# Second attention: each head's query and key halves stacked in 128 rows, one product pair and one wait per head

## The chip, the cores and the metric

One NeuronCore of a Trainium2 chip runs the whole program. The metric is the device time in microseconds (us) of one execution; lower is better. TensorE is written PE (PEld for its weight loads), VectorE DVE, ScalarE ACT, GpSimd POOL, and SP is the engine that issues most transfers.

## What is computed

The reference is two transformer blocks on 512 tokens of width 1024. The change lies in the attention of the second block (`fox_attention`), with 16 heads of size 64:

```python
def fox_attention(h, w_in, b_f, w_out):
    proj = h @ w_in
    q, k, v = ...                       # 16 heads of 64, from proj
    q = q * jnp.asarray(HEAD_DIM_2 ** -0.5, q.dtype)
    f_logit = (proj[..., 3 * D:] + b_f).astype(jnp.float32)
    log_f = jax.nn.log_sigmoid(f_logit)
    c = lax.cumsum(log_f, axis=1).transpose(0, 2, 1)
    ...
        s = jnp.einsum('bhqd,bhkd->bhqk', qb, k, preferred_element_type=jnp.float32)
        s = s + cb[..., :, None] - c[..., None, :]
        s = jnp.where(k_pos[None, :] <= q_pos[:, None], s, NEG_INF)
        pr = jax.nn.softmax(s, axis=-1)
    ...
    return o @ w_out
```

The term `cb` is the same for all keys of a query, so softmax drops it. The kernel adds only the sums of the gate that belong to the keys (`c`).

## The kernel before

Every matrix product is made of three products of rounded parts: a value is split into a "hi" part (fp32r) and a "lo" rest, and hi*hi + hi*lo + lo*hi are added in PSUM. Weights come in 352 transfers of 512 KB, one for each unit of 128 x 1024: SP loads it into `w_raw`, ACT rounds it into `w_hi` (function `highs`), POOL subtracts to get `w_lo`, and PE multiplies (lines 519 to 521, helper `three`). A unit fills one PSUM bank. All engines run hand-written instruction lists that wait on counting semaphores, so the order in the code is the order on each engine.

The second attention works on 8 pairs of heads, `fox_pair(p)`, one for each 128 output columns. Units `fox + 3p`, `+1`, `+2` make q, k and v of pair p. They are made ahead, in the gaps of earlier pairs: `more(i)` (or `fill`) puts the table `FOX_FILL[p][i]` pieces of 3 products of 128x512 between the steps of the attention. When a unit is complete, ACT and DVE evict it at the same index i, in `fox_evict(p, i)`: DVE multiplies by the inverse norm (`fox_scaled`), ACT writes the hi part (`fox_high`, after one weight rounding by `highs`), and DVE writes the lo part at its next `evict` (`fox_low`). By the table q of a later pair is evicted in pairs 0 (i = 3), 1 (3), 2 (5), 3 (7), 4 (10) and 6 (0), k in pairs 0 (7), 1 (9), 3 (0), 4 (1), 5 (2) and 6 (4), and v of the last pair at the very end of pair 6 (i = 11). Units 3 to 5 are complete before pair 0 starts.

In a pair, the scores of query block qi (0 to 3) against (qi + 1) x 128 keys go to PSUM bank 2 for head 0 and bank 3 for head 1 (`scores(qi)`). The two heads lie in rows 0 to 63 and 64 to 127 of the same tiles. There are four products with 64 rows for each head: q_hi k_hi, q_hi k_lo, q_lo k_hi, and ones with `c_head`, which holds the gate's sums of the pair in one row of each half. Then a causal mask is added by a product with the identity (line 984). DVE takes the row maxima (`peak`, line 1320), ACT the exponentials with their sums (`exps`, line 1991), DVE divides (`normalise`). PE turns the probabilities (line 1000), ACT and DVE split them (`fpt_hi`, `fpt_lo`), and PE multiplies them by v (`pv`, lines 1007 to 1009). `head_rows(p)` on DVE writes `c_head` of the next pair after the last `normalise`. `CREDIT` is a start value of 2 on some semaphores. Pair 7 has no units to make; it fills with pieces of the output product (`fill_out`).

Ahead of pair 0, ACT and DVE work out the gate: the absolute value, exponential and logarithm on ACT, the running sum `c_rows` on DVE, mixed with the first q, k and v.

## Time and profile before

| what | value |
|---|---|
| three runs | 2181.66 us median, 2180.15 to 2186.51 |
| the profiled execution | 2185.68 us, span 2183.9 us |
| PE busy | 2146.1 us, 98% of the span |
| DVE, ACT, POOL busy | 1013.6, 869.6, 933.8 us |
| mean granted TensorE clock | 0.994 |
| weight transfers | 352 of 512 KB, 3.5 us each to landing |

PE is busy nearly all the time, so the program's length is PE's instruction list plus the holes in it. The second attention lies between about 885 and 1115 us of the span. The first score product of the eight pairs starts at 900.86, 928.87, 955.92, 982.08, 1008.58, 1034.51, 1061.87 and 1088.33 us.

### The profile page before, as it was taken

The page shows a single profiled execution, that of the slowest core. Times are in us where ns is not written, and L with a number is a line of the kernel's source. Part 1 is how long each engine was busy: PE and PEld are TensorE (multiplying, and loading weights), DVE is VectorE, ACT ScalarE, POOL GpSimd, SP SyncE. Part 2 cuts the span into 40 slices and gives each one's busy share as a digit, 9 for nine tenths or more (in the row PEclk, how much of TensorE's full clock was granted, in tenths as well). Part 3 has the DMA queues.
Part 4 walks back from the last instruction along what each step waited for, and adds up shares of the span by engine and source line. Part 5 has one row for each costly group of instructions (what it writes and reads, how often), then busy time and mean ns, then how long its engine had stood idle before and what let it go on. Part 6 is the DMA issues. An engine that isn't in the chain of part 4 may idle for free.

```text
span 2183.9 us, 25305 instructions
## 1 busy us (share of the span) xinstructions
PE 2146.1 (98%) x10192; PEld 1758.8 (81%) x10192; DVE 1013.6 (46%) x1637; ACT 869.6 (40%) x1358; POOL 933.8 (43%) x424
## 2 busy tenths in 40 slices
PE   9999999999999999999999999999999999999998
PEld 7877778888888887777778888888888888888886
DVE  5877775445524235666634422313653345122134
ACT  5434346444424254444434422324532244233234
POOL 5722124434444455322225444444554454444446
PEclk9999999999999999999999999999999999999999
DMA  4421112233233332211122333322223323332222
GB/s 159 148 75 41 47 49 80 94 97 106 97 97 97 97 115 78 70 57 49 49 67 88 97 97 97 97 97 87 97 87 97 97 85 99 97 97 96 97 80 85
DMA packets 53829, 193.27 MB, mean 88 GB/s; under 512 B 6096, under 2 KB 6224, under 8 KB 53712
## 3 DMA queue, kind: packets, MB, share of 16 engines
q1 hardware_dynamic: 52992, 189.81, 27.0%
q10 hardware_dynamic: 720, 1.84, 0.3%
q8 instruction: 81, 1.33, 0.2%
q14 instruction: 36, 0.29, 0.0%
HBM read 189.53 MB, written 2.10 MB: 88 GB/s over the span
## 4 chain that ended last, share of the span: by engine, by line
PE 89%; DVE 6%; ACT 3%; issue 1%; DMA 0%; POOL 0%; DVEq 0%; ACTq 0%; POOLq 0%
PE ps L519 27%; PE ps L521 27%; PE ps L520 27%; PE ps L733 1%; DVE ps L1209 1%; PE ps L982 1%; PE ps L713 1%; PE ps L1000 1%; PE ps L725 1%; ACT w_hi L1855 1%; PE ps L615 1%; DVE xg_lo L1169 1%; PE ps L1007 0%; DVE ps L1730 0%; PE ps L715 0%
## 5 line engine op out<-in xcount | busy, mean ns | idle before, releaser
L472 POOL TENSOR_TENSOR w_lo<-w_raw,w_hi 128x1024 fp32r<-128x1024 f32 x352 | 852.6, 2424 | 1211.4 <-ACT w_hi L1855 1211.3
L519 PE MATMUL ps<-xg_hi,w_hi 128*128 128x512 f32 x1688 | 674.1, 399 | 5.4 <-POOL w_lo L486 2.8
L521 PE MATMUL ps<-xg_hi,w_lo 128*128 128x512 f32 x1688 | 661.2, 392 | 0.0
L520 PE MATMUL ps<-xg_lo,w_hi 128*128 128x512 f32 x1688 | 660.7, 391 | 0.0
L1855 ACT ACTIVATE w_hi<-w_raw 128x1024 fp32r<-128x1024 f32 x352 | 372.3, 1058 | 626.5 <-PE ps L521 623.8
L519 PEld LDWEIGHTS ps<-xg_hi,w_hi 128*128 128x128 f32 x1688 | 318.8, 189 | 69.3 <-issue 3.0
L521 PEld LDWEIGHTS ps<-xg_hi,w_lo 128*128 128x128 f32 x1688 | 318.5, 189 | 67.9
L520 PEld LDWEIGHTS ps<-xg_lo,w_hi 128*128 128x128 f32 x1688 | 319.2, 189 | 59.4
L521 PE MATMUL ps<-h_hi,w_lo 128*128 128x512 f32 x688 | 267.8, 389 | 0.0
L519 PE MATMUL ps<-h_hi,w_hi 128*128 128x512 f32 x688 | 267.8, 389 | 0.0
L520 PE MATMUL ps<-h_lo,w_hi 128*128 128x512 f32 x688 | 267.8, 389 | 0.0
L1143 DVE TENSOR_TENSOR ps<-ps,inv_rms 128x512 f32<-128x512 f32 x164 | 113.6, 696 | 194.2 <-PE ps L521 181.1
L521 PEld LDWEIGHTS ps<-h_hi,w_lo 128*128 128x128 f32 x688 | 129.2, 188 | 26.9
L520 PEld LDWEIGHTS ps<-h_lo,w_hi 128*128 128x128 f32 x688 | 129.2, 188 | 26.7
L519 PEld LDWEIGHTS ps<-h_hi,w_hi 128*128 128x128 f32 x688 | 129.2, 188 | 26.6
L1499 DVE TENSOR_TENSOR mixed<-mixed,ps 128x512 f32<-128x512 f32 x48 | 33.0, 688 | 199.9 <-PE ps L521 199.9
L1169 DVE SCALAR_TENSOR_TENSOR xg_lo<-resid,vec,xg_hi 128x512 fp32r<-128x512 f32 x72 | 85.5, 1191 | 12.7 <-ACT xg_hi L1881 12.5
L1209 DVE SCALAR_TENSOR_TENSOR ps<-glu,vec,ps 128x512 f32<-128x512 f32 x116 | 87.1, 751 | 1.9
L1844 ACT ACTIVATE h_hi<-ps 128x512 fp32r<-128x512 f32 x86 | 51.5, 598 | 90.1 <-DVE ps L1761 48.8
L1881 ACT ACTIVATE xg_hi<-resid,vec 128x512 fp32r<-128x512 f32 x72 | 51.7, 717 | 62.7 <-DVE resid L1499 40.2
L481 POOL TENSOR_TENSOR sq_sum<-sq_sum,sq 128x512 f32<-128x512 f32 x42 | 66.2, 1577 | 23.7 <-ACT sq L1878 21.4
L1761 DVE TENSOR_TENSOR ps<-tile_b,ps 128x512 f32<-128x512 f32 x64 | 44.6, 696 | 57.7 <-ACT tile_b L2296 57.7
(342 smaller groups left out, 2462.7 us busy)
## 6 DMA issues: line engine op xcount, KB each, us to landing
w_raw<-in_weights SPq DMA_DIRECT2D x352, 512.0 KB, 3.5
out_x<-mixed SPq DMA_DIRECT2D x8, 256.0 KB, 2.1
resid<-in_x SPq DMA_DIRECT2D x3, 512.0 KB, 7.4
p_raw<-in_p ACTq DMA_DIRECT2D x3, 512.0 KB, 3.6
resid<-in_x SPq DMA_DIRECT2D x2, 256.0 KB, 4.0
last_gain<-in_last_gain SPq DMA_DIRECT2D x1, 512.0 KB, 4.6
w_raw<-in_weights SPq DMA_DIRECT2D x1, 256.0 KB, 4.0
w_raw<-in_weights ACTq DMA_DIRECT2D x1, 256.0 KB, 4.4
```

The costliest lines, as they stand in the source:

```text
L472: pool.tensor_tensor(w_lo[:, slot, :], w_raw[:, u % RAW, :], w_hi[:, slot, :].bitcast(F32), ALU.subtract).then_inc(w_ready, 1)
L481: pool.tensor_tensor(sq_sum[:], sq_sum[:], sq[:, m % 2:m % 2 + 1, :], ALU.add).then_inc(summed, 1)
L519: pe.matmul(o, w, x, start=start, stop=False)
L520: pe.matmul(o, w, xl, start=False, stop=False)
L521: return pe.matmul(o, wl, x, start=False, stop=stop)
L1143: dve.tensor_tensor(out, ps[:, BANK[u]:BANK[u] + 1, :], R[:], ALU.mult).then_inc(done, 1)
L1169: dve.scalar_tensor_tensor(xg_lo[:, m:m + 1, :], X[:, m:m + 1, :], g, xg_hi[:, m:m + 1, :].bitcast(F32), ALU.mult, ALU.subtract).then_inc( ...
L1209: ins = dve.scalar_tensor_tensor(acc if k < CONV_TAPS - 1 else conv_acc[:, ct, :], src, w, acc, ALU.mult, ALU.add)
L1761: dve.tensor_tensor(t, T2[:, m % 2:m % 2 + 1, :], t, ALU.mult).then_inc(s_mlp["s"], 1)
L1844: act.activation(out, x, ACT.Copy, scale=scale).then_inc(done, 1)
L1855: act.activation(w_hi[:, u % RING, :], w_raw[:, u % RAW, :], ACT.Copy).then_inc(w_hi_ready, 1)
L1881: act.activation(xg_hi[:, m:m + 1, :], X[:, m:m + 1, :], ACT.Copy, scale=g).then_inc(prep_hi, 1)
```

## The change

For each head there is a stack of 128 rows. In `fq[.., hd, t]` the head's own 64 rows hold q_hi for both t = 0 and t = 1; the other 64 rows hold ones for t = 0 and q_lo for t = 1. In `fk[.., hd, t]` the own rows hold k_hi (t = 0) and k_lo (t = 1); the other rows hold the gate's sums (t = 0) and a copy of k_hi (t = 1). Product t = 0 is q_hi k_hi plus ones times sums, product t = 1 is q_hi k_lo plus q_lo k_hi. So a head has two products with 128 rows instead of four with 64. Each head's products and mask now stand together and wait for the exponentials of that head alone.

To fill the stacks, ACT writes q_hi as two instructions of 64x1024 and k_hi as two of 64x512, and issues two transfers that copy k_hi to the other half (128 KB each, two for each pair, at the place of the v unit). DVE writes q_lo, k_lo and the gate's sums as two instructions of 64 rows each. The ones are written once by four ACT instructions ahead of the gate. There is no `c_head`; its content lies in the double-buffered `fk`.

```diff
-            for n, (first, base) in enumerate(((0, 0), (32, 0), (64, -1), (96, -1))):
+            for n, (first, base) in enumerate(((0, -1), (32, -1), (64, 0), (96, 0))):
...
                 def scores(qi):
                     e, n = 8 * p + 2 * qi, (qi + 1) * P
-                    pe.wait_ge(A2["exps"], e + 2)
                     qs = slice(qi * P, n)
-                    for t, (a, b) in enumerate(((q[0][:, qs], k[0]), (q[0][:, qs], k[1]), (q[1][:, qs], k[0]), (ones_r, c_head))):
-                        for hd in range(2):
-                            rows = slice(hd * HD, (hd + 1) * HD)
-                            pe.matmul(ps[:, 2 + hd, 0:n], a[rows, :], b[rows, 0:n], start=t == 0, stop=False)
                     for hd in range(2):
+                        pe.wait_ge(A2["exps"], e + hd + 1)
+                        for t in range(2):
+                            pe.matmul(ps[:, 2 + hd, 0:n], fq[:, par, hd, t, qs], fk[:, par, hd, t, 0:n], start=t == 0, stop=False)
                         pe.matmul(ps[:, 2 + hd, qs], ident_r[:], causal_r[:], start=False, stop=True).then_inc(A2["scores"], 1)
...
-                pe.wait_ge(A2["crow"], p + 1)
+                pe.wait_ge(A2["qklo"], 2 * p + 2)
+                pe.wait_ge(A2["crow"], 2 * p + 2)
+                pe.wait_ge(A2[f"kdup{par}"], 32 * (p // 2 + 1))
+                if p == 0:
+                    pe.wait_ge(A2["ones"], 4)
                 scores(0); more(0)
...
             def fox_low(n):
                 if which == 0:
-                    dve.wait_ge(A2["qkhi"], 2 * p + 1)
-                    dve.scalar_tensor_tensor(fq_lo[:, par:par + 1, :], bank(u0 + n), HD ** -0.5, fq_hi[:, par:par + 1, :].bitcast(F32),
-                                             ALU.mult, ALU.subtract).then_inc(bank_free, 1)
+                    dve.wait_ge(A2["qkhi"], 4 * p + 2)
+                    for hd, done in ((0, A2["qklo"]), (1, bank_free)):
+                        rows, other = (slice(h * HD, (h + 1) * HD) for h in (hd, 1 - hd))
+                        dve.scalar_tensor_tensor(fq[other, par, hd, 1, :], ps[rows, BANK[u0 + n], :], HD ** -0.5,
+                                                 fq[rows, par, hd, 1, :].bitcast(F32), ALU.mult, ALU.subtract).then_inc(done, 1)
...
             def head_rows(p):
-                dve.tensor_scalar(c_head[:], c_rows[:], head_sel[:, p:p + 1], None, ALU.mult).then_inc(A2["crow"], 1)
+                for hd in range(2):
+                    other = slice((1 - hd) * HD, (2 - hd) * HD)
+                    dve.tensor_scalar(fk[other, p % 2, hd, 0, :], c_rows[other, :], head_sel[other, p:p + 1], None,
+                                      ALU.mult).then_inc(A2["crow"], 1)
...
             def fox_high(n):
                 highs(u0 + n + 1 + RING)
                 if which < 2:
                     act.wait_ge(A2["qk"], 2 * p + which + 1)
-                    copy_hi((fq_hi, fk_hi)[which][:, par:par + 1, :], bank(u0 + n), A2["qkhi"], (HD ** -0.5, 1.0)[which])
+                for hd in range(2):
+                    rows, other = (slice(h * HD, (h + 1) * HD) for h in (hd, 1 - hd))
+                    if which == 0:
+                        copy_hi(fq[rows, par, hd, :, :], ps[rows, BANK[u0 + n], :].unsqueeze(1).to_broadcast([HD, 2, S]), A2["qkhi"], HD ** -0.5)
+                    elif which == 1:
+                        copy_hi(fk[rows, par, hd, 0, :], ps[rows, BANK[u0 + n], :], A2["qkhi"])
+                    else:
+                        if hd == 0:
+                            act.wait_ge(A2["qkhi"], 4 * p + 4)
+                        act.dma_start(fk[other, par, hd, 1, :].bitcast(F32), fk[rows, par, hd, 0, :].bitcast(F32)).then_inc(A2[f"kdup{par}"], 16)
+            for par in range(2):
+                for hd in range(2):
+                    other = slice((1 - hd) * HD, (2 - hd) * HD)
+                    copy_hi(fq[other, par, hd, 0, :].rearrange("p (a b) -> p a b", b=P), ones[other, :].unsqueeze(1).to_broadcast([HD, QB, P]),
+                            A2["ones"])
             taken(U["forget"])
```

On PE, before, `scores(3)` of pair 0 stands like this, behind the pieces of `more(2)` (a row's number is its place on the engine; the shapes printed are those of the output):

```order
3947 L521 MATMUL ps<-xg_hi,w_lo 128x512
3948 L982 MATMUL ps<-fk_hi,fq_hi 128x512 [waits fox_exps]
3949 L982 MATMUL ps<-fk_hi,fq_hi 128x512
3950 L982 MATMUL ps<-fk_lo,fq_hi 128x512 x2
3951 L982 MATMUL ps<-fk_hi,fq_lo 128x512 x2
3952 L982 MATMUL ps<-c_head,ones_r 128x512 x2
3953 L984 MATMUL ps<-causal_r,ident_r 128x128 x2
3954 L519 MATMUL ps<-xg_hi,w_hi 128x512
```

The same place of the changed kernel:

```order
3947 L518 MATMUL ps<-xg_hi,w_lo 128x512
3948 L977 MATMUL ps<-fk,fq 128x512 [waits fox_exps]
3949 L977 MATMUL ps<-fk,fq 128x512
3950 L978 MATMUL ps<-causal_r,ident_r 128x128
3951 L977 MATMUL ps<-fk,fq 128x512 [waits fox_exps]
3952 L977 MATMUL ps<-fk,fq 128x512
3953 L978 MATMUL ps<-causal_r,ident_r 128x128
3954 L516 MATMUL ps<-xg_hi,w_hi 128x512
```

Eight products of half height for both heads have become four of full height, and head 0's mask stands ahead of head 1's products.

On ACT, before, from the end of the norm that precedes the stage up to the first exponentials of pair 0 (`inv_rms` is the norm, `logf` the gate, `fprob` the probabilities):

```order
508 L1889 ACTIVATE inv_rms<-ps 128x512 [waits norm_broadcast]
509 L2217 ACTIVATE logf<-logf,vec 128x512 [waits bank_free]
510 L2219 ACT_TABLE_LOAD
511 L2219 ACTIVATE logf<-logf 128x512 [waits forget_act]
512 L1844 ACTIVATE fq_hi<-ps 128x512 [waits fox_qk]
513 L1844 ACTIVATE fk_hi<-ps 128x512 [waits fox_qk]
514 L2223 ACT_TABLE_LOAD
515 L2223 ACTIVATE logf<-logf,ones 128x512 [waits forget_act]
516 L2226 ACTIVATE c_hi<-c_rows 128x512 [waits forget_dve]
518 L1844 ACTIVATE fq_hi<-ps 128x512 [waits fox_qk]
520 L1844 ACTIVATE fk_hi<-ps 128x512 [waits fox_qk]
523 L1991 ACTIVATE fprob,fstat<-ps,fstat 128x128 [waits fox_peak] x2
```

And of the changed kernel, up to the gate's logarithm and the first two transfers:

```order
508 L1894 ACTIVATE inv_rms<-ps 128x512 [waits norm_broadcast]
509 L1849 ACTIVATE fq<-ones 64x512 x4
510 L2236 ACTIVATE logf<-logf,vec 128x512 [waits bank_free]
511 L2238 ACT_TABLE_LOAD
512 L2238 ACTIVATE logf<-logf 128x512 [waits forget_act]
513 L1849 ACTIVATE fq<-ps 64x1024 [waits fox_qk]
514 L1849 ACTIVATE fq<-ps 64x1024
515 L1849 ACTIVATE fk<-ps 64x512 [waits fox_qk]
516 L1849 ACTIVATE fk<-ps 64x512
518 L2242 ACTIVATE logf<-logf,ones 128x512 [waits forget_act]
519 L2227 DMA fk<-fk 64x512 [waits fox_qkhi]
520 L2227 DMA fk<-fk 64x512
```

Four instructions for the ones stand ahead of the gate's first step, and the first q and k, ahead of its last step, have become four longer or equal ones.

On ACT at the border of pairs 6 and 7, in the changed kernel (before, the same rows stood there without the two transfers):

```order
687 L1849 ACTIVATE fo_hi<-ps 64x512 [waits fox_pv]
688 L1860 ACTIVATE w_hi<-w_raw 128x1024 [waits w_loaded2,unit_done]
689 L2227 DMA fk<-fk 64x512 [waits fox_qkhi]
690 L2227 DMA fk<-fk 64x512
691 L1996 ACTIVATE fprob,fstat<-ps,fstat 128x128 [waits fox_peak] x2
```

The transfers for pair 7 stand behind a weight rounding that waits for the last unit PE makes in pair 6.

## Rows read from the trace of the kernel before

**Rows 1.** The page's chain that ended last, by engine.

```profile
PE 89%; DVE 6%; ACT 3%; issue 1%; DMA 0%; POOL 0%; DVEq 0%; ACTq 0%; POOLq 0%
```

**Rows 2.** Windows: busy us and instructions by engine, clock, pair 2.

```profile
955.80:982.00 26.20, 26.20 (x152) 20.71 (x151) 16.20 (x40) 12.07 (x31) 6.45 (x3) 1.00 0.20 61
```

**Rows 3.** Timeline of PE, pair 2, `scores(3)`: start, duration, engine, line.

```profile
964.26 0.39 PE L521 MATMUL ps<-xg_hi,w_lo 128*128 128x512 f32 x1
964.58 0.50 PE L982 MATMUL ps<-fk_hi,fq_hi 64*128 64x512 f32 x2
964.91 0.39 PE L982 MATMUL ps<-fk_lo,fq_hi 64*128 64x512 f32 x2
965.15 0.40 PE L982 MATMUL ps<-fk_hi,fq_lo 64*128 64x512 f32 x2
...
965.98 0.45 PE L519 MATMUL ps<-xg_hi,w_hi 128*128 128x512 f32 x1
```

**Rows 4.** Timeline of PE, pair 2, rows on both sides of `scores(0)`.

```profile
955.36 0.39 PE L520 MATMUL ps<-xg_lo,w_hi 128*128 128x512 f32 x1
955.59 0.40 PE L521 MATMUL ps<-xg_hi,w_lo 128*128 128x512 f32 x1
...
956.78 0.45 PE L519 MATMUL ps<-xg_hi,w_hi 128*128 128x512 f32 x1
```

**Rows 5.** Timeline of PE, pair 2: products of full height with 128 columns.

```profile
975.00 0.28 PE L1008 MATMUL ps<-fpt_lo,fv_hi 128*128 128x128 f32 x1
975.11 0.28 PE L1009 MATMUL ps<-fpt_hi,fv_lo 128*128 128x128 f32 x1
```

**Rows 6.** Groups by line and form, 898 to 1110 us.

```profile
L1855 ACT ACTIVATE w_hi<-w_raw 128x1024 fp32r<-128x1024 f32 x20 | 21.2, 1059 | 6.0 <-PE ps L521 5.9
...
L1149 DVE TENSOR_TENSOR fo_lo<-ps,fo_hi 64x512 fp32r<-64x512 f32 x14 | 9.6, 683 | 11.3 <-ACT fo_hi L1844 11.2
...
L1844 ACT ACTIVATE fo_hi<-ps 64x512 fp32r<-64x512 f32 x15 | 8.8, 587 | 8.8 <-PE ps L1009 8.8
...
L1652 DVE TENSOR_SCALAR c_head<-c_rows,head_sel 128x512 fp32r<-128x512 f32 x7 | 3.4, 481 | 0.0
```

**Rows 7.** Timeline of ACT, the gate and the start of pair 0.

```profile
885.02 0.72 ACT L2217 ACTIVATE logf<-logf,vec 128x512 f32<-128x512 f32 x1 [0.76 <-DVE logf L1629]
...
900.97 1.06 ACT L1855 ACTIVATE w_hi<-w_raw 128x1024 fp32r<-128x1024 f32 x1 [0.97 <-PE ps L521]
902.04 1.28 ACT L1991 ACT_TABLE_LOAD   x1
903.34 0.37 ACT L1991 ACTIVATE fprob<-ps,fstat 128x128 f32<-128x128 f32 x1
```

**Rows 8.** Timeline of PE: `scores(1)` of pair 0.

```profile
904.20 0.39 PE L982 MATMUL ps<-fk_hi,fq_hi 64*128 64x256 f32 x2 [0.87 <-ACT fprob L1991]
```

**Rows 9.** Timeline of PE: a wait in the first attention.

```profile
127.83 0.41 PE L752 MATMUL ps<-cmp_mask_r,ident_r 128*128 128x128 f32 x2 [4.06 <-DVE vc_lo L1149]
```

**Rows 10.** Windows, the columns of group 2: the stretch behind that wait.

```profile
127.80:138.00 10.20, 10.17 (x50) 8.18 (x50) 3.85 (x10) 3.13 (x7) 0.00 (x0) 0.53 0.15 58
```

**Rows 11.** Timeline of PE: waits in pairs 0 and 5.

```profile
917.89 0.50 PE L1007 MATMUL ps<-fpt_hi,fv_hi 128*128 128x512 f32 x1 [0.88 <-DVE fpt_lo L1149]
...
1038.28 0.39 PE L982 MATMUL ps<-fk_hi,fq_hi 64*128 64x256 f32 x2 [1.30 <-ACT fprob L1991]
```

**Rows 12.** Timeline of ACT: the weight rounding between pairs 6 and 7.

```profile
1088.43 1.06 ACT L1855 ACTIVATE w_hi<-w_raw 128x1024 fp32r<-128x1024 f32 x1 [0.16 <-PE ps L521]
```

**Rows 13.** Timeline of ACT's queue: issue of another transfer.

```profile
446.66 0.34 ACTq L2104 DMA_DIRECT2D p_raw<-in_p  x1
```

**Rows 14.** The page's DMA issues: KB each, median us from issue to landing.

```profile
out_x<-mixed SPq DMA_DIRECT2D x8, 256.0 KB, 2.1
```

**Rows 15.** Timeline of PE: waits in pair 7.

```profile
1089.87 0.47 PE L519 MATMUL ps<-fo_hi,w_hi 128*128 128x512 f32 x1 [0.51 <-DVE fv L1143]
...
1097.45 0.49 PE L982 MATMUL ps<-fk_hi,fq_hi 64*128 64x512 f32 x2 [0.37 <-ACT fprob L1991]
```

More of the change, by code:

```diff
@@ L314, in build @@
         with ExitStack() as fx:
-            fq_hi = sb("fq_hi", [P, 2, S], F32R, fx)
-            fq_lo = sb("fq_lo", [P, 2, S], F32R, fx)
-            fk_hi = sb("fk_hi", [P, 2, S], F32R, fx)
-            fk_lo = sb("fk_lo", [P, 2, S], F32R, fx)
+            fq = sb("fq", [P, 2, 2, 2, S], F32R, fx)
+            fk = sb("fk", [P, 2, 2, 2, S], F32R, fx)
             fv = sb("fv", [P, 1, S], scope=fx)
@@ L331, in build @@
             c_hi = sb("c_hi", [P, S], F32R, fx)
-            c_head = sb("c_head", [P, S], F32R, fx)
         with ExitStack() as c3:
@@ L374, in build @@
         s_cs = stage_sems("cmp_att", "scores", "sub", "exp", "stat", "probs")
-        A2 = stage_sems("fox", *att_names, "qk", "qkhi", "vturned", "vhi", "vlo", "crow")
+        A2 = stage_sems("fox", *att_names, "qk", "qkhi", "vturned", "vhi", "vlo", "crow", "qklo", "kdup0", "kdup1", "ones")
         s_fg = stage_sems("forget", "dve", "act")
@@ L971, in fox_pair @@
                 par = p % 2
-                q, k = (fq_hi[:, par, :], fq_lo[:, par, :]), (fk_hi[:, par, :], fk_lo[:, par, :])
                 def scores(qi):
                     e, n = 8 * p + 2 * qi, (qi + 1) * P
-                    pe.wait_ge(A2["exps"], e + 2)
                     qs = slice(qi * P, n)
-                    for t, (a, b) in enumerate(((q[0][:, qs], k[0]), (q[0][:, qs], k[1]), (q[1][:, qs], k[0]), (ones_r, c_head))):
-                        for hd in range(2):
-                            rows = slice(hd * HD, (hd + 1) * HD)
-                            pe.matmul(ps[:, 2 + hd, 0:n], a[rows, :], b[rows, 0:n], start=t == 0, stop=False)
                     for hd in range(2):
+                        pe.wait_ge(A2["exps"], e + hd + 1)
+                        for t in range(2):
+                            pe.matmul(ps[:, 2 + hd, 0:n], fq[:, par, hd, t, qs], fk[:, par, hd, t, 0:n], start=t == 0, stop=False)
                         pe.matmul(ps[:, 2 + hd, qs], ident_r[:], causal_r[:], start=False, stop=True).then_inc(A2["scores"], 1)
@@ L1618, in fox_low @@
                 if which == 0:
-                    dve.wait_ge(A2["qkhi"], 2 * p + 1)
-                    dve.scalar_tensor_tensor(fq_lo[:, par:par + 1, :], bank(u0 + n), HD ** -0.5, fq_hi[:, par:par + 1, :].bitcast(F32),
-                                             ALU.mult, ALU.subtract).then_inc(bank_free, 1)
+                    dve.wait_ge(A2["qkhi"], 4 * p + 2)
[3 more added lines that the diff above has]
+                                                 fq[rows, par, hd, 1, :].bitcast(F32), ALU.mult, ALU.subtract).then_inc(done, 1)
                 elif which == 1:
-                    dve.wait_ge(A2["qkhi"], 2 * p + 2)
-                    low(fk_lo[:, par:par + 1, :], bank(u0 + n), fk_hi[:, par:par + 1, :], bank_free)
+                    dve.wait_ge(A2["qkhi"], 4 * p + 4)
+                    for hd, done in ((0, A2["qklo"]), (1, bank_free)):
+                        rows = slice(hd * HD, (hd + 1) * HD)
+                        low(fk[rows, par, hd, 1, :], ps[rows, BANK[u0 + n], :], fk[rows, par, hd, 0, :], done)
             uu = U["forget"]
```

## The prediction

> **What bounds the kernel now.** First the chain that ended last: 89% of the span is PE [rows 1]. So time is won only where PE's own list gets shorter or a hole in it closes, and lost where a hole opens. Then the windows of one pair of the second attention: PE is busy 26.20 of 26.20 us while ACT works 12.07 and DVE 16.20 [rows 2]. The other engines have idle time on the average; whether they have it where the change puts work is to be read at each place. There the timeline shows a list so well balanced that small waits are already there: 0.87 us before scores(1) of pair 0 [rows 8], 0.88 before the first product with v of pair 0, 1.30 in pair 5 [rows 11], 0.51 and 0.37 in pair 7 [rows 15]. At those places ACT or DVE ends last, and anything added to them costs its full length.
>
> **PE's list (a gain).** The four products of a head have 64 rows, but the two heads run beside each other: two products of 512 columns (x2) advance the timeline by 0.24 us, from 964.91 to 965.15 [rows 3], hardly more than one product of full height does (0.23, from 955.36 to 955.59 [rows 4]). So halving the number of products with double height gives no fewer columns in time: four pair steps before, four full steps after. What goes is the change of shape. scores(3) with the mask takes 965.98 - 964.26 = 1.72 us including the L521 ahead of it, which is worth 0.23; so 1.49 [rows 3]. After: 4 x 0.23 for the products, 2 x 0.11 for the masks (a product of 128 columns steps by 0.11 [rows 5]), 0.05 for the extra turn from small to large, 1.19. Saved 0.30. scores(0): 956.78 - 955.59 - 0.23 = 0.96 before [rows 4], 6 x 0.11 = 0.66 after; saved 0.30 too. I take 0.30 for all 32: **-9.6 us**. Bounds: 0, if steps of full height with these operands are slower than those of the rows, and -13, if the masks hide too.
>
> **Prices of what is added.** On ACT an instruction of 1024 columns takes 1.06 us and one of 512 columns 0.59, of which about 0.1 overlaps with the next; half the rows make it no shorter (64x512 in 587 ns) [rows 6]. So q costs 2 x 0.96 in place of 0.5: +1.4. k costs 2 x 0.5 in place of 0.5: +0.5. On DVE 64x512 takes 683 ns, as long as 128 rows: +0.6 for q_lo and +0.6 for k_lo. The gate's sums take 481 ns an instruction, two for one: +0.4. No row shows ACT reading PSUM twice over by a broadcast; the nearest is the 1024-column row from SBUF, and I take it. Its lower bound is that of one 512-column instruction for each half, +0.5.
>
> **The start of pair 0 (a loss).** The gate's chain alternates between ACT and DVE and ends in the sums. ACT sits idle for 0.76 us before its first step [rows 7]; the four ones instructions take 1.9, so the chain is 1.1 late. The first q and k stand between the exponential and the logarithm: +1.4 +0.5, so the sums are 3.0 late. Behind them DVE has one more sums instruction (+0.4), ACT the q of pair 1 (+1.4) and its k (+0.5); a wait of 0.97 that ACT had at 900.97 [rows 7] swallows 1.0. In all the first exponential moves from 903.34 by 3.0 + 0.4 + 1.4 + 0.5 - 1.0 = 4.3 to 907.6. scores(1) started at 904.20, after a wait of 0.87 [rows 8]. Now it needs only the exponentials of head 0, 0.35 sooner than both, so it starts at 908.1, 3.9 later; and the 0.3 that scores(0) saves is lost in the wait as well: **+4.2**. PE stands still for over 5 us there (0.87 + 3.9 + 0.3). The sums themselves come just in time for scores(0), since they were some 3 us early.
>
> The clock: after PE's wait of 4.06 us at 127.83 [rows 9] the granted clock of the next 10.2 us was 0.53, so the array ran at the lower of its two levels, 1.2 GHz [rows 10]. The wait in pair 0 would be longer than that one. Behind it PE has dense work, so I take a short low stretch, of which some falls into the wait: **+1.0**, with 0 and +5 (half of 10.2) as ends. The Trainium skill, "TensorE: Matmul & The Clock Gate", Part 1, says that the array's clock is halved when it has been idle and given back under load; by that rule the low stretch is certain, by the row it is likely.
>
> **The evictions in pairs 0 to 6.** Six q's and six k's are evicted between steps of the attention. A visit costs PE what it adds to the chain of exponentials, turned probabilities and lo parts, less the slack there. Two are worked out. Pair 0: fq_hi stands, by the order in `fox_pair`, right ahead of the first fpt_hi, and PE waits 0.88 for what follows [rows 11]. Added: 1.4 for q and 0.4 for the sums; taken back: 0.8, since head 0's scores are ready earlier and both exponentials start sooner; and PE arrives 0.3 earlier. So the wait grows by 1.4 + 0.4 - 0.8 + 0.3 = 1.3. Pair 1 has q at the same index: 1.3. At the border of pairs 4 and 5 q stands ahead of the last fo_hi, and the wait of 1.30 [rows 11] follows: 1.4 on ACT and 0.6 on DVE, less 0.3 for waiting on one head only: 1.7. The others (pairs 2, 3, 6) I put near 1.1 each, an estimate between 0 and 2.4. Sum for q, 1.3 + 1.3 + 1.7 + 3 x 1.1 = **+7.6**, ends 0 and 14. A k adds 0.5 on ACT and 0.6 on DVE, at indexes with a few tenths of slack: 0.7 each, **+4.2**, ends 0 and 6.6.
>
> **The copies of k.** They are issued with v, which for pairs 2 to 6 is many pieces ahead: hidden. For pair 7 they stand behind the rounding at 1088.43, which waits for PE's last piece [rows 12]. An issue holds ACT's queue for 0.34 us and does not wait for the engine's instruction to end (it lies beside one) [rows 13]. So the second goes out at 1088.8. Nothing shows a transfer of 128 KB inside SBUF; the nearest is 256 KB in 2.1 us [rows 14]. Landing at 1090.9; PE wanted scores(0) at 1088.3: +2.6. Back come the 0.51 and 0.37 of waits in pair 7 that then lie behind [rows 15] and 0.8 by the earlier exponentials of the last block: **+0.9**, ends -1 and +3. By the Trainium skill, "DMA: Bandwidth & Descriptors", Anatomy of one DMA, some 2.0 us are fixed and the bytes add 0.3; with its 2.3 the sum would be 0.2 higher.
>
> **Sum.** -9.6 + 4.2 + 1.0 + 7.6 + 4.2 + 0.9 = **+8.3 us**. The profiled execution took 2185.68 and would take 2194.0; against the median of the runs, 2181.66, that gives 2190. The profiled one was 4 us above the median, inside the spread of the runs, so the difference carries over and not the level.
>
> **Rivals.** (a) *The idle time of ACT and DVE takes the evictions* (faster). 12.07 of 26.20 us busy [rows 2] speaks for it, the existing waits at the very places against. Then -9.6 + 4.2 + 1.0 + 0.9 = -3.5, 2178; with half of the start's 5.2 hidden as well, -6.1, 2175.6. It decides from the point where a visit costs less than 0.3 us on the average.
> (b) *More waits than counted* (slower still): low clock for 10 us behind pair 0's wait (+5 in place of +1), and q at its upper end (+14 in place of 7.6): +18.7, 2200. The low clock of [rows 10] speaks for it; that PE has dense pieces behind the wait speaks against it.
> (c) *The full-height products save nothing*: steps of fq and fk as slow as the blocks before, gain 0: +17.9, 2199.6. The steps of [rows 5] speak against it.
> (d) *The change is about even*: the start costs 2 in place of 5.2 and evictions 9: 9 + 2 + 0.9 - 9.6 = +2.3, 2184.
>
> **How the numbers follow.** Forecast (2184 to 2196) 0.53, (a) 0.22, (b) 0.09, (c) 0.05, (d) 0.11. A measurement here tells 0.3%, 6.5 us, from no change: below 2175.1 is faster, above 2188.2 slower. Of (a) half lies below 2175.1: 0.11 faster. Of the forecast two thirds lie above 2188.2, with (b) and (c): 0.35 + 0.14 = 0.49 slower. The rest, 0.40, is the same. The range 2178 to 2198 leaves out the lower half of (a) and most of (b) and (c). The likeliest case's own range is 2184 to 2196.
>
> **What the next profile would show.** PE: blocks of two heads 0.3 us shorter, from the piece ahead to the piece behind; a wait of about 5 us before scores(1) of pair 0, put down to the exponentials, and a granted clock under 1 behind it; the waits before the first product with v in pairs 0 and 1 near 2.2; scores(1) of pair 5 waiting about 3; scores(0) of pair 7 waiting some 2.6 for a landing. ACT: q as 2 x 1.06. All pairs 1 to 6 near 26 us again. What would make it wrong: ACT instructions from PSUM with a broadcast far from 1.06; other phases than thought between PE and ACT, so that visits fall in real gaps; landings far above 2.1.

## The result, and the profile after

| | before | after |
|---|---|---|
| median of 5 runs each | 2181.66 us | 2212.02 us (2211.23 to 2224.84) |
| ratio | | 1.0145, 95% interval 1.0129 to 1.0161 |
| profiled execution, span, mean granted clock | 2185.68, 2183.9 us, 0.994 | 2224.84, 2223.1 us, 0.984 |
| mean granted clock of the other four runs | | 0.988 to 0.990 |

The change makes the kernel slower by 1.45%, some 30 us, where +8.3 was forecast with 2198 as the upper end. The profiled execution is the slowest of the five, 13 us above the median; what is read from it below may overstate the loss, the clock's part above all.

The chain that ended last, by engine (before: [rows 1]): PE has lost 4 points to DVE and ACT.

```profile
PE 85%; DVE 8%; ACT 5%; issue 1%; DMA 0%; POOL 0%; DVEq 0%; ACTq 0%; POOLq 0%
```

Now the whole second attention in one window, from the first piece after the norm to the first piece of the output product that waits for the last fo_lo. First the kernel before (us, then busy us and instructions of PE, PEld, DVE, ACT, POOL, then the granted clock):

```profile
884.32:1114.78 230.46, 219.62 (x1251) 173.26 (x1251) 146.21 (x335) 111.12 (x261) 52.57 (x22) 1.00 0.16 51
```

And the kernel after, with stretches of 15 us at its start:

```profile
886.67:1153.02 266.35, 226.92 (x1123) 186.54 (x1123) 163.04 (x359) 131.10 (x281) 52.57 (x22) 0.93 0.18 52
895.00:910.00 15.00, 9.14 (x43) 7.28 (x41) 11.61 (x15) 8.47 (x10) 4.44 (x2) 0.92 0.21 52
910.00:925.00 15.00, 14.04 (x66) 11.96 (x67) 11.58 (x30) 7.71 (x20) 4.36 (x3) 0.85 0.31 88
925.00:940.00 15.00, 10.33 (x46) 8.45 (x45) 7.60 (x12) 6.44 (x11) 2.02 (x2) 0.77 0.12 36
955.00:970.00 15.00, 11.80 (x59) 9.75 (x58) 7.78 (x16) 6.74 (x12) 2.36 (x1) 0.89 0.16 54
```

The stage is 35.9 us longer. PE's idle time in it went from 10.8 (230.46 - 219.62) to 39.4 us: +28.6. Its busy time rose by 7.3, although the list is shorter; with 32 blocks of 0.31 us saved (measured below, 9.9 us) PE was busy 17.2 us more than its list needs, which is the work at the lower clock. Outside of the stretches at the lower clock the granted clock is 1.00; there are eight of them in the stage, some 37 us in all, and in each it is 0.50, the lower of the two levels. So the profiled loss is -9.9 + 28.6 + 17.2.

Six of the 25 waits on PE's timeline (in brackets: how long, and what ended it); of those left out the longest are 2.21 us in pair 3 and 2.01 in pair 6:

```profile
904.56 0.41 PE L977 MATMUL ps<-fk,fq 128*128 128x128 f32 x2 [1.28 <-issue]
...
910.96 0.77 PE L516 MATMUL ps<-xg_hi,w_hi 128*128 128x512 f32 x1 [5.54 <-DVE fk L1147]
...
930.49 0.80 PE L1001 MATMUL ps<-fpt_hi,fv_hi 128*128 128x512 f32 x1 [4.67 <-DVE fpt_lo L1147]
...
961.53 0.50 PE L1001 MATMUL ps<-fpt_hi,fv_hi 128*128 128x512 f32 x1 [3.19 <-DVE fpt_lo L1147]
...
1068.10 0.77 PE L977 MATMUL ps<-fk,fq 128*128 128x256 f32 x2 [3.50 <-ACT fprob L1996]
...
1126.26 0.66 PE L977 MATMUL ps<-fk,fq 128*128 128x128 f32 x2 [3.12 <-DMA fk<-fk]
```

They answer to [rows 11] and [rows 15]: the 0.88 before the first product with v in pair 0 is 4.67, the 1.30 in pair 5 is 3.50. The 0.87 of [rows 8], before scores(1), is gone: PE now waits ahead of it. The 5.54 stands at a place that had no wait, the first piece of `more(0)`, whose bank is held by k of pair 1 until DVE has written its lo part.

Why so late, on DVE (start, duration, what it waited for):

```profile
901.34 3.01 DVE L1656 TENSOR_SCALAR fk<-c_rows,head_sel 64x512 fp32r<-64x512 f32 x2
904.28 1.28 DVE L1141 TENSOR_TENSOR ps<-ps,inv_rms 128x512 f32<-128x512 f32 x2
907.09 1.41 DVE L1620 SCALAR_TENSOR_TENSOR fq<-ps,fq 64x512 fp32r<-64x512 f32 x2 [1.53 <-ACT fq L1849]
909.40 1.41 DVE L1147 TENSOR_TENSOR fk<-ps,fk 64x512 fp32r<-64x512 f32 x2 [0.90 <-ACT fk L1849]
...
923.38 3.01 DVE L1656 TENSOR_SCALAR fk<-c_rows,head_sel 64x512 fp32r<-64x512 f32 x2
```

And POOL beside it:

```profile
900.90 2.66 POOL L469 TENSOR_TENSOR w_lo<-w_raw,w_hi 128x1024 fp32r<-128x1024 f32 x1 [12.30 <-ACT w_hi L1860]
...
923.53 2.58 POOL L469 TENSOR_TENSOR w_lo<-w_raw,w_hi 128x1024 fp32r<-128x1024 f32 x1 [10.64 <-ACT w_hi L1860]
```

The two instructions for the sums take 3.01 us where w_lo lies beside them and 1.00 elsewhere; single ones take 477 to 2501 ns. ACT's rows at the same place: the ones 2.60 us, the first q 2.05, its k 1.21, and the first exponential at 911.84, against 903.34 in [rows 7]; counted from the stage's start that is 6.15 us later.

```profile
886.64 2.60 ACT L1849 ACTIVATE fq<-ones 64x512 fp32r<-64x512 f32 x4
...
905.00 2.06 ACT L1849 ACTIVATE fq<-ps 64x1024 fp32r<-64x1024 f32 x2 [4.17 <-DVE ps L1141]
...
909.40 1.12 ACTq L2227 DMA_DIRECT2D fk<-fk  x2
...
911.84 0.37 ACT L1996 ACTIVATE fprob<-ps,fstat 128x128 f32<-128x128 f32 x1
```

### The profile page after: what moved, and what is told of

It reads as the page before. It is cut to its first block, busy times and chain, and to the rows that moved or that the text cites. A ratio compares the mean times of both kernels' runs of the same rounds, so it can differ in the third digit from the quotient of the medians.

```text
span 2223.1 us, 25118 instructions
## 1 busy us (share of the span) xinstructions
PE 2157.1 (97%) x10064; PEld 1774.9 (80%) x10064; DVE 1031.3 (46%) x1661; ACT 889.8 (40%) x1378; POOL 933.4 (42%) x424
## 4 chain that ended last, share of the span: by engine, by line
PE 85%; DVE 8%; ACT 5%; issue 1%; DMA 0%; POOL 0%; DVEq 0%; ACTq 0%; POOLq 0%
PE ps L516 26%; PE ps L518 25%; PE ps L517 25%; PE ps L730 1%; DVE ps L1207 1%; PE ps L710 1%; ACT w_hi L1860 1%; ACT fq L1849 1%; PE ps L722 1%; DVE fprob L1327 1%; ACT fprob L1996 1%; PE ps L612 1%; PE ps L994 1%; PE ps L1001 1%; DVE xg_lo L1167 1%
## 5 line engine op out<-in xcount | busy, mean ns | idle before, releaser
L478 POOL TENSOR_TENSOR sq_sum<-sq_sum,sq 128x512 f32<-128x512 f32 x42 | 66.5, 1584 | 24.5 <-ACT sq L1883 22.2
L1156 DVE TENSOR_TENSOR sq_sum<-sq_sum,ps 128x512 f32<-128x512 f32 x57 | 39.1, 686 | 69.6 <-ACT ps L1877 69.4
```

The source lines that it names most:

```text
L478: pool.tensor_tensor(sq_sum[:], sq_sum[:], sq[:, m % 2:m % 2 + 1, :], ALU.add).then_inc(summed, 1)
L1156: dve.tensor_tensor(sq_sum[:], sq_sum[:], ps[:, NB:NB + 1, :], ALU.add).then_inc(summed, 2 if m == DC - 2 and in_two_parts(n) else 1)
```

## The experiments

Each kernel ran beside the kernel before on its chip; its ratio to before is what is compared, with 95% intervals, and 0.001 is 2.2 us. The changed kernel stands at 1.0145 (1.0129 to 1.0161). Two theories at first: the work that the change adds on ACT and DVE makes PE wait, and the waits bring the low clock (A); or the new form of the products, with its waits per head, does it by itself (B).

**The added work taken out.** q_hi once from pair 2 on, sums and copies of k for two pairs only, ones on GpSimd:

```diff
-                if p < 7:
-                    head_rows(p + 1)
+                if p == 0:
+                    head_rows(1)
...
-                    if which == 0:
+                    if which == 0 and p > 1:
+                        copy_hi(fq[rows, par, hd, 0, :], ps[rows, BANK[u0 + n], :], A2["qkhi"], HD ** -0.5)
+                    elif which == 0:
```

> The changed kernel with the work that it adds on ACT and DVE taken out of the pairs: q_hi is written once (64x512 twice) after pair 1, the gate's sums are written for pairs 0 and 1 only, k_hi is copied for pairs 0 and 1 only, and the ones are written by GpSimd. So it computes with stale sums and stale copies of k_hi and q_hi from pair 2 on. Theory A (the added work on ACT and DVE makes TensorE wait, and the waits bring the low clock): only the shorter lists of the score blocks are left, 0.35 to 0.40 us in each of 32, so about 12 us under the kernel before less what the start of pair 0 still costs (1 to 3 us): 2170 to 2175 us, ratio 0.995 to 0.997, clock 0.993 or more. Rival B (the full-height products, with the waits that stand per head, are what lowers the clock and opens the holes, whatever ACT and DVE do): 2200 us or more, clock 0.990 or less. Between the two, 2180 to 2195, both have a part.

Measured: 2194.44 us, ratio 1.0055 (1.0040 to 1.0071). 20 us of the loss went, but it is still slower than before: the time falls between the spans of A and B, so this run alone leaves a part to both. Its waits show where the rest is: 5.29 and 3.90 us in pair 0, where its work had not been taken out, and 2.65 and 2.18 in pairs 5 and 6 (before 1.30 and 1.76), with ACT and DVE still writing 64 rows at a time. The clock of the stage was 0.97.

**Only q's work, on the kernel before.**

```diff
-                    copy_hi((fq_hi, fk_hi)[which][:, par:par + 1, :], bank(u0 + n), A2["qkhi"], (HD ** -0.5, 1.0)[which])
+                    for hd in range(2):
+                        rows = slice(hd * HD, (hd + 1) * HD)
+                        copy_hi(fq_hi[rows, par, hd, :, :], ps[rows, BANK[u0 + n], :].unsqueeze(1).to_broadcast([HD, 2, S]), A2["qkhi"], HD ** -0.5)
```

> The kernel before, with its eight products of half height and one wait per score block, but with ACT's q work of the changed kernel (two instructions of 64x1024, the second copy is not read) and DVE's q_lo as two instructions of 64 rows. It computes the same. Theory A: the longer evictions alone bring waits where a border or a full-bank point follows (terms put at +7.6 before), and low clock behind them: 5 to 15 us slower than before, 2187 to 2197, ratio 1.002 to 1.007. Rival B (the waits come from the per-head order and the copies, not from q's evictions): 2180 to 2184, ratio 1.000 to 1.001.

Measured: 2201.73 us, 1.0083 (1.0070 to 1.0096), 18 us, more than A's upper end. Only q's evictions and the place that they write differ from before, so this is the cleanest price of a term. The stage in its trace, and 15 us of it with one wait:

```profile
877.41:1128.45 251.04, 228.88 (x1251) 179.53 (x1251) 151.61 (x343) 123.30 (x269) 52.49 (x22) 0.96 0.15 47
...
945.00:960.00 15.00, 12.93 (x67) 10.86 (x69) 7.07 (x14) 6.56 (x13) 2.20 (x2) 0.89 0.11 36
```

20.6 us longer than before: 11.3 of idle time (22.2 for 10.8) and 9.3 of busy time, with the same 1251 products. The lower clock took nearly as much as the waits. And the waits themselves:

```profile
916.84 0.70 PE L1009 MATMUL ps<-fpt_hi,fv_hi 128*128 128x512 f32 x1 [2.48 <-DVE fpt_lo L1151]
...
947.07 0.50 PE L1009 MATMUL ps<-fpt_hi,fv_hi 128*128 128x512 f32 x1 [2.48 <-DVE fpt_lo L1151]
...
980.14 0.33 PE L1009 MATMUL ps<-fpt_hi,fv_hi 128*128 128x128 f32 x1 [1.61 <-DVE fpt_lo L1151]
...
1047.76 0.58 PE L984 MATMUL ps<-fk_hi,fq_hi 64*128 64x256 f32 x2 [3.49 <-ACT fprob L1996]
```

Against 0.88 and 0.89 (pairs 0 and 1), nothing (pair 2) and 1.30 before: +1.60, +1.59, +1.61 and +2.19. The waits of pairs 3 and 6 grow by 1.37 and 1.49. So the six visits cost 9.9 us of waits, each about what q's evictions are longer by, and the start 1.5 more (2.32 before the first piece behind scores(0), for 0.87 before scores(1)).

**The wait per head.** `e + hd + 1` became `e + 2` again.

> The changed kernel in which each head's products wait for the exponentials of both heads, as before, with the new products and their order kept. It computes the same. Theory A (the added work): no change beyond 2 us, 2210 to 2216, since the waits of TensorE that the profile shows at scores() are for a transfer, an eviction or the row maxima, which both forms wait for. Rival C (the wait per head starts head 0 early and so moves the row maxima and the exponentials into worse places): 5 us or more faster, 2207 or less. Should the wait per head be worth something, 3 to 6 us slower: 2215 to 2218.

Measured: 2217.13 us, 1.0153 (1.0140 to 1.0167): the interval overlaps that of the changed kernel. The wait per head neither costs nor gives what a run here can tell; rival C falls.

**PE kept busy in its waits.** Products that nobody reads are put into the waits. Two runs; the edit of the second:

```diff
-                scores(0); more(0)
+                scores(0)
+                if p == 0:
+                    spin(20, 4)
+                more(0)
...
-                turn(0, 0); turn(0, 1); more(4); pv(0, 0)
+                turn(0, 0); turn(0, 1); more(4); spin({0: 18, 1: 12}.get(p, 0), 6); pv(0, 0)
```

> The changed kernel with 22 products more in front of scores(1) of pair 0, 18 and 12 in front of the first pv of pairs 0 and 1, into banks that nobody reads then, so that TensorE works through the two longest waits of the profile after (5.54 and 3.19 us) and most of 4.67. It computes the same. Theory A1 (the low clock behind the waits costs as much as the waits themselves): the two or three low stretches in pairs 0 and 1, 6.8 us each with half of it lost, go: 7 to 10 us less than the changed kernel if the products only fill the waits, 2203 to 2206, clock up by 0.003 to 0.005. Rival A2 (the low clock comes from somewhere else than the waits, from the kind of product): the time rises by what the products take beyond the waits, 2212 to 2218, and the clock stays at 0.988 to 0.990.

Measured: 2219.80 us, 1.0166 (1.0152 to 1.0180). The 22 products stood behind the wait of 5.54 us and only lengthened the list, so the sum was a mixture, and it decides nothing. With the first group in the wait:

> The changed kernel with products more, into banks that nobody reads then: 20 between scores(0) and more(0) of pair 0, where the profile after shows the wait of 5.54 us, 18 and 12 in front of the first pv of pairs 0 and 1, where it shows 4.67 and 3.19 us. It computes the same. At 0.226 us each (the steps of the rows of 128x512) they fill 4.5, 4.1 and 2.7 us and should overrun no wait, so the time can only change by the clock. In the earlier run with 22, 18 and 12 the 22 stood behind the longest wait and not in it, 5 us of list more. Theory A1 (the low clock behind a wait costs about as much as the wait): the stretches of 0.92, 0.85, 0.77 and 0.89 in 895 to 970 us of the profile after, 8.5 us together, go for the most part: 5 to 9 us under the changed kernel, ratio 1.0105 to 1.0125. Rival A2 (the low clock has another cause): ratio 1.014 to 1.016, the clock unchanged.

Measured: 2213.81 us, 1.0129 (1.0113 to 1.0144), 3.5 us under the changed kernel. That is less than A1 expected, lies between A1 and A2, and the intervals overlap. In its trace the stretches at the start have no low clock:

```profile
895.00:910.00 15.00, 12.78 (x64) 10.18 (x63) 10.49 (x18) 9.02 (x13) 7.39 (x3) 1.00 0.28 87
910.00:925.00 15.00, 14.86 (x71) 11.80 (x69) 11.02 (x23) 7.62 (x17) 2.59 (x1) 1.00 0.26 72
925.00:940.00 15.00, 13.53 (x74) 11.13 (x75) 9.24 (x19) 6.72 (x17) 2.39 (x1) 1.00 0.09 35
```

Up to the same row in pair 2 it takes 86.0 us (882.95 to 968.98), the changed kernel 90.5 (886.67 to 977.17): 4.5 us came back there, with 50 products more in the list. Five stretches at the lower clock are left in the stage, all behind waits that were not filled. That the low clock follows the waits is shown; that filling waits with such products pays as a whole is not.

**Pairs 0 and 1 in the form of before**, the others stacked.

> The changed kernel with pairs 0 and 1 in the form of before: their q, k and sums in 128-row instructions, eight products of half height, one wait per score block, no copies of k_hi; pairs 2 to 7 as changed, the ones written by GpSimd in pair 0. It computes the same. Theory A (the start at pair 0 is the largest part of the loss: in the profile after, the waits of 5.54, 4.67, 3.19 and 1.28 us in pairs 0 and 1, against 0.87, 0.88 and 0.89 us before, and the clock of 0.77 to 0.94 that follows them, about 6 us): 12 + 6 - 3 (two pairs less with the short list) = 15 us under the changed kernel, so near 2198 us, ratio 1.006 to 1.010, clock 0.991 or more. Rival (the waits only move to pairs 2 and 3, because what is late there is the same added work): 2206 us or more, ratio 1.012 or more.

Measured: 2209.11 us, 1.0102 (1.0085 to 1.0119). 9 us of the 15 came, and the ratio lies between the theory and the rival. The 5.54 is gone, but pair 0's wait before v is still 2.47 and pair 1's 3.11 (3.19 in the changed kernel), since the q of a stacked pair is evicted right ahead of it. In pair 0:

```profile
914.98 2.06 ACT L1881 ACTIVATE fq<-ps 64x1024 fp32r<-64x1024 f32 x2 [0.93 <-DVE ps L1162]
917.07 0.98 ACT L1881 ACTIVATE fpt_hi<-ps 128x512 fp32r<-128x512 f32 x2
```

**Single pieces of the added work.** q_hi written once from pair 2 on:

> The changed kernel in which ACT writes q_hi once (64x512 twice, 1.21 us, for 64x1024 twice, 2.06 us) from pair 2 on; its second place keeps the values of pairs 0 and 1, so the products t = 1 of pairs 2 to 7 are computed with an old q_hi. Theory A (q's evictions keep TensorE waiting, my term of +7.6 us with 1.1 to 1.7 us for each): half of it, 0.85 us in each of the six pairs or less, with the low clock behind it, 3 to 7 us under the changed kernel: 2206 to 2210 us. Rival (the evictions are covered; only the start costs): within 1.5 us of the changed kernel, 2212 to 2215.

Measured: 2211.62 us, 1.0120 (1.0105 to 1.0135), -5.5 us. The sums for two pairs only:

> The changed kernel in which DVE writes the gate's sums for pairs 0 and 1 only; the later pairs use those of pairs 0 and 1. Left out are 12 instructions of 64x512 at 0.86 us in the mean (up to 2.50 us beside GpSimd's w_lo). Theory A (they stand between the last normalise and the split of the turned probabilities, for which pv waits): before spent 0.5 us there and the changed kernel 1.0 to 3.0, so 0.5 to 2.5 us in some of six pairs, with clock 3 to 8 us under the changed kernel: 2205 to 2210. Rival (fpt_lo waits for ACT's fpt_hi and not for them): within 1.5 us, 2212 to 2215.

Measured: 2212.09 us, 1.0120 (1.0104 to 1.0135), -5.5 us. By the ratio both lie in A's span, but both intervals overlap that of the changed kernel by a little, so -5.5 us is a rough price. The traces are clearer: without the second q_hi the waits of pairs 2 and 5 are 0.74 and 2.65 for 1.61 and 3.50, without the sums pair 1's is 2.29 for 3.19 and the 2.21 in pair 3 is gone. The copies issued at k's own place:

> The changed kernel with the two transfers of k_hi issued on ACT right behind k_hi's own eviction, not at the place of the v unit. It computes the same. Theory A (pair 7's copies are late: its first score waits 3.12 us for the transfer, with low clock behind it): 3 to 5 us under the changed kernel, 2208 to 2211 us. Rival (the issue, 1.1 us of ACT's queue for two, now stands ahead of a pair's exponentials and costs there what it saves at pair 7): within 1.5 us, 2212 to 2215, or slower.

Measured: 2223.95 us, 1.0177 (1.0162 to 1.0192), 7 us slower, as the rival had it. Pair 7's wait is gone, but the issue (two in 1.12 us of ACT's queue) stands ahead of exponentials in six pairs; at 1009.30 the first of them starts 1.20 us after the engine's last work, put down to the issue. Of PE's waits:

```profile
1009.92 0.61 PE L977 MATMUL ps<-fk,fq 128*128 128x384 f32 x2 [1.65 <-ACT fprob L1996]
...
1045.06 0.73 PE L977 MATMUL ps<-fk,fq 128*128 128x512 f32 x2 [1.52 <-ACT fprob L1996]
```

where the changed kernel waited 0.48 and less than 0.3.

**Copies and stacks by transfers on SP's queue.** If A is right, the form pays once ACT and DVE have their old work. First only the copies; then the whole stacks, with q and k evicted as before into a tile `fs` (pairs 0 and 1 unstacked in both, the sums moved among the splits `lo(0, 2)` and `lo(0, 3)`):

```diff
+                n = u - U["fox"] - RING - RAW - 1
+                if 3 * PLAIN <= n < 24 and n % 3 < 2:
+                    p, which, par = n // 3, n % 3, n // 3 % 2
+                    sp.wait_ge(bank_free, U["fox"] + n + 1)
...
+                            moves = ((fq[rows, par, hd, 0, :], hi), (fq[rows, par, hd, 1, :], hi), (fq[other, par, hd, 1, :], lo))
...
+                            moves = ((fk[rows, par, hd, 0, :], hi), (fk[other, par, hd, 1, :], hi), (fk[rows, par, hd, 1, :], lo))
+                        for o, i in moves:
+                            sp.dma_start(o.bitcast(F32), i).then_inc(A2[("qs", "ks")[which] + str(par)], 16)
```

> Pairs 0 and 1 in the form of before. From pair 2 on the stacks stay, but ACT writes q_hi once (64x512 twice) and issues no transfer: SP's queue copies q_hi to its second place and k_hi to the other half, behind the weight transfers; DVE writes the gate's sums among the splits of the turned probabilities and not between the last normalise and them. It computes the same. From the runs so far, theory A (each piece of added work on ACT and DVE costs its length in waits and clock): 1.0102 of the kernel with pairs 0 and 1 as before, less 0.0025 for q_hi, less 0.0022 for the sums, less 0.0015 for pair 7's wait of 3.13 us: ratio 1.003 to 1.005, 2192 to 2196 us. Rival (the transfers delay the weights or land late): 1.008 or more. Second rival (all the loss was in these pieces and the short list of six pairs shows, -9 us): 0.999 or less.

> As the run beside it, but from pair 2 on ACT and DVE write q and k exactly as in the kernel before (one instruction of 128x512 for each hi and lo part, into a tile beside the stacks), and SP's queue builds the stacks by twelve transfers of 128 KB for each pair. DVE's work is that of before but for the sums (64x512 twice), ACT's is that of before. It computes the same. Theory A (the loss is the added work on ACT and DVE): what is left is the short list, 24 blocks of 0.37 us, 9 us, less the waits for exponentials that a shorter list uncovers (7 us more of them than before stood in the pairs 2 to 7 of the run with the added work off, which still had half of it): ratio 0.996 to 1.001, 2176 to 2188 us. Rival (the stacked form itself costs, by its waits for the exponentials and the clock behind them, whatever ACT and DVE do): 1.003 or more. Rival (1.5 MB more of transfers for each pair delay the weights): waits for w_hi or w_lo on TensorE, 1.005 or more.

Measured: 2206.79 us, 1.0100 (1.0086 to 1.0113), and 2195.42 us, 1.0051 (1.0038 to 1.0064). Both miss A's span. The first is its rival's case, the transfers land late; the second lies where both of its rivals put it, but by the same cause. In the second kernel, on PE and on SP's queue:

```profile
1060.87 0.66 PE L1011 MATMUL ps<-fk,fq 128*128 128x128 f32 x2 [3.63 <-DMA fk<-fs]
...
1099.35 0.66 PE L1011 MATMUL ps<-fk,fq 128*128 128x128 f32 x2 [10.80 <-DMA fk<-fs]
```

```profile
1068.64 12.38 SPq L409 DMA_DIRECT2D w_raw<-in_weights  x2
1081.06 3.69 SPq L438 DMA_DIRECT2D fq<-fs  x6
1092.08 0.33 SPq L409 DMA_DIRECT2D w_raw<-in_weights  x1
1092.46 3.68 SPq L438 DMA_DIRECT2D fk<-fs  x6
```

The transfers for pair 7 go out at 1092.46, when the weight ahead of them got its slot, and pair 7 had been waiting since 1088.6. So it was their place in the queue, which neither expectation named. One weight earlier in the queue (`n = u - U["fox"] - RING - RAW`), three kernels:

> The kernel in which SP's transfers build the stacks of pairs 2 to 7, with these transfers one weight earlier in SP's queue, so that they no longer stand behind a weight whose slot comes free only at the end of the pair. It computes the same. Theory A (the stacked form saves its 9 us of list in 24 blocks once ACT and DVE work as before): the waits of 3.63 and 10.80 us and the clock behind them (0.80 and 0.66 in two stretches of 15 us, 8 us, of which part stood in the waits) go, 18 to 21 us under the 2195 us of that run: 2174 to 2178 us, ratio 0.995 to 0.998. Rival (the transfers land late wherever they are queued, as they take long behind weights of 512 KB): a wait of 2 us or more stays at pair 6 or 7, ratio 0.999 or more. Rival (new waits for the exponentials take the gain): ratio 0.999 to 1.001 with no wait for a transfer.

> As the run beside it, with pair 1 stacked too, so that only pair 0 has the form of before; the ones are written by GpSimd ahead of pair 0. It computes the same. Theory A: four more blocks of 0.35 us, 1 to 2 us under the run beside it, and nothing at the start, where ACT and DVE do what they did: ratio 0.001 lower at most. Rival (the transfers for pair 1 fall into the busy start and delay weights or the start of pair 0): 2 us or more above the run beside it.

> The kernel in which SP's transfers make the second q_hi and the copies of k_hi while ACT writes q_hi and k_hi by 64x512 twice and DVE the lo parts likewise, with the transfers one weight earlier in the queue. It computes the same. Theory A (each added instruction on ACT and DVE costs its length, with the clock behind it): the waits of 1.80 and 9.13 us and their clock go, 15 us under its first run: ratio 1.002 to 1.004, 5 to 8 us above the first kernel of this batch per what ACT (0.6 us each for q and k) and DVE (0.7 us each) still do more in six pairs. Rival (half-height evictions are covered, only q's double write and the transfers cost): within 2 us of the first kernel of this batch.

| kernel | us | ratio to before |
|---|---|---|
| stacks by transfer, in time | 2179.09 | 0.9970 (0.9957 to 0.9982) |
| pair 1 stacked too | 2178.51 | 0.9967 (0.9956 to 0.9979) |
| copies by transfer, in time | 2191.86 | 1.0031 (1.0022 to 1.0040) |

The first two are faster than the kernel before, by 6 to 7 us, with the stacked form and a wait per head: B falls. By the ratio the first lies within its span. The two can't be told apart. The stage of the second, then those of the first and the third, and 15 us of the third around its longest wait:

```profile
883.62:1106.78 223.16, 210.87 (x1138) 174.74 (x1138) 150.70 (x342) 111.34 (x261) 55.52 (x26) 1.00 0.38 102
...
881.70:1106.74 225.04, 212.28 (x1154) 174.27 (x1154) 150.60 (x341) 111.33 (x261) 55.10 (x26) 1.00 0.35 94
...
879.72:1116.82 237.10, 214.61 (x1155) 173.91 (x1155) 156.51 (x353) 118.86 (x273) 55.02 (x26) 1.00 0.23 63
1030.00:1045.00 15.00, 12.38 (x69) 10.47 (x68) 8.96 (x23) 5.96 (x17) 2.39 (x1) 1.00 0.25 75
```

Against before, the second has 8.75 us less of PE's busy time at the same clock, which over 28 blocks is 0.31 each, and 1.5 us more idle time. ACT's 111.34 us are those of before. The waits for exponentials that I feared a shorter list would uncover are 0.82, 1.30 and 1.75 where before had 0.56, 1.30 and 1.76. The third kernel of the table keeps the eviction by halves (ACT 118.9 us, DVE 156.5). It lies 0.0061, 13 us, above the first, which stacks the same pairs; 5 to 8 us were expected. In the profiles PE's idle time is 22.5 us for 12.8, at the same clock. The two differ in the eviction by halves and in the number of transfers, of which the third has the fewer; so the evictions are what divides a gain from a loss.

## Why the prediction was wrong

The direction was right and so were most of the mechanisms. The stage of the profiled execution grew by 35.9 us where +8.3 was forecast: the list gave back 9.9 for 9.6, the waits cost 28.6 for 16.9 (4.2 + 7.6 + 4.2 + 0.9), and the clock 17.2 for 1.0. So two steps failed: the clock was priced for one wait, and the waits were too small together.

- *PE's list, -9.6.* Right: 0.31 us in a block, -9.9 for 32. Rival (c) falls.
- *"The clock: +1.0".* The step that failed most. I read one wait of 4.06 us with 10.2 us at 0.53 behind it [rows 9, 10], and then let a single short low stretch stand, since PE has dense work behind the wait. Dense work did not spare it, and there was not one such stretch but eight, behind waits of 5.54, 4.67, 3.50, 3.19, 3.12, 2.21 and 2.01 us and one behind two waits of 1.06 and 0.45. In the profiled run it cost 17.2 us. In the other four, an estimate from the mean clock (0.988 to 0.990 for 0.994 of some 2200 us) gives 9 to 13. Every term that makes a wait should have been charged with a clock share. By the kernel with q's work that share was 9.3 us on 11.3 of waits. It is no fixed share, and the length of the wait alone does not settle it: in that kernel the clock fell at waits of 2.32 and 2.48 us, while the kernel with the copies in time held 1.00 through 22.5 us of idle time and a wait of 2.62 (its last row above). What decides between them stays open. The Trainium skill, "TensorE: Matmul & The Clock Gate", Part 1, was cited for the rule that an idle array loses half its clock: the trace agrees (0.50 in each of the eight stretches), and I gave the rule too little weight.
- *The start of pair 0, +4.2.* From the stage's first row to scores(1) it is 26.99 us for 19.88, +7.1. Two links were missing. The sums start 4.2 us late and end 4.7 late (3.0 forecast: the ones took 2.6 us and not 1.9, and the first q and k add 2.2 and not 1.9), which is more than the 3.5 us of slack before scores(0), so PE waits 1.28 there; and the piece behind scores(0) needs the bank that k of pair 1 holds. I followed the exponentials and not the bank.
- *"The gate's sums: +0.4".* The 481 ns of [rows 6] is the mean of those that lie alone. Beside POOL's w_lo one instruction takes 2.50 us; the trace before has one too (2.51 at 894.82), which I had not looked up. At 923.38 that is 2.1 us more than forecast on the way to pair 0's first product with v, and most of what makes the wait 4.67 and not 2.2; the same happens in pair 3 (2.21, gone in the run without the sums). In pair 1 the two took 1.00 us with no w_lo beside them, and 0.9 of its 3.19 went with them. The Trainium skill, "SBUF — State Buffer", Who interferes with whom, says that such a DVE instruction and a GpSimd instruction take one pair of ports in turn, and that the second one stands still until the first is done; the rows above fit that, with w_lo ending at 926.1 and the DVE pair, which began before it, only at 926.4.
- *q's evictions, +7.6.* The mechanism was right and the size low: in the kernel with q's work the six visits cost 9.9 us of waits, 1.6 for each of pairs 0, 1 and 2, 1.4 and 1.5 in pairs 3 and 6 and 2.2 in pair 5, where I had 1.3, 1.3, 1.1, 1.1, 1.1 and 1.7. I had assumed slack in pairs 2, 3 and 6, of which there was hardly any. I had also taken back 0.8 in pair 0 for earlier exponentials of head 0; with one wait for both heads pair 0's wait before v is 4.63 for 4.67, so that gain did not come.
- *k's evictions, +4.2, and the copies, +0.9.* No run takes k's evictions alone, so their term stays open. Pair 7's wait is 3.12 for 2.6 forecast. The issue of two transfers holds ACT's queue for 1.12 us, not 0.68 as [rows 13] had it, and they land in 2.3 us in the median, where I took 2.1 and had an estimate of 2.3 from the Trainium skill, "DMA: Bandwidth & Descriptors", Anatomy of one DMA. That section gives its figures for transfers issued by GpSimd and these went out on ACT's queue, so the agreement shows no more than these numbers. The 0.51 and 0.37 came back, but of the 0.8 for the last block only 0.33 (a wait of 0.52 for 0.85): pair 7 lost 1.9 us.

Rival (b), more waits than counted, was the true case and had 0.09; even its 2200 was too low, since it let only pair 0's wait lower the clock. Rival (a) fell at its own point: a visit of q costs 1.4 to 2.2 us, not under 0.3. Rival (d) put the start and the evictions lower still and fell with it.

What stays open: how the 20 us between the changed kernel and the one with the added work off divide between waits and clock in the median run, since single executions differ by up to 13 us and by 0.006 in the mean clock; at which waits the clock falls; and whether filler products would pay in the final form, which wasn't tried.

## What to carry to other kernels

On a list where PE is busy 98% of the time, price an added instruction on another engine twice: its full length at each place where PE already waits a little, and up to as much again for the clock where the wait grows to some microseconds (9.3 us on 11.3 here). Halving the rows of an eviction left its time as it was (0.6 us on ACT for 64x512 and for 128x512), so put data into an odd layout by transfers rather than by extra instructions, if the consumer is a stage away; then ask what stands ahead of the transfer in its queue. And for every duration taken from a group, look at its longest member and what lay beside it.

## What was not expected of the hardware

- A stage with waits of 3 to 5.5 us ran at a mean granted clock of 0.93 although PE was busy for 226.92 of 266.35 us; in stretches of 15 us at its start with such a wait in them or just ahead it was 0.77 to 0.92. At a wait of 2.32 us it fell in one kernel, at one of 2.62 in another it did not.
- DVE's scaling of 64x512 from SBUF took up to 2.50 us beside w_lo on POOL and 0.48 alone.
- Transfers of 128 KB inside SBUF landed in 2.3 us (median, 2.2 to 3.5) from ACT's queue and in 3.0 to 4.6 us (medians of five kernels) from SP's queue among weights; twelve more for each pair (a DMA share of 0.38 in the stage for 0.16) brought no wait for a weight in the stage. Six issues took 3.7 us of SP's queue.
- Products of 64 rows for two heads step through 512 columns in 0.24 us, nearly as fast as one of 128 rows (0.23); the gain of stacking is 0.31 us in a block of 0.96 to 1.49 and comes, it seems, from the short products and the changes of shape, which was not tried apart.
